# Moving a ScalarE weight split behind the next round's exponentials in a fused two-block transformer kernel

## The reference

```
h = rms_norm(x); z = h @ w_in                       # 1024 -> 5632
o_a = dilated_mixer(...)    # 6 heads, three dilations, softmax over a window
o_b = moba_attn(...)        # 6 heads, causal softmax
o_m = memory_attn(...)      # 4 heads on 256 memory tokens
gates = sigmoid(z[..., o3:])                        # 3 x 1024 columns of z
y = gates[0]*(o_a @ w_pa) + gates[1]*(o_b @ w_pb) + gates[2]*(o_m @ w_pm)
x = x + y @ w_o
x = x + square(relu(rms_norm(x) @ w_up)) @ w_down
```

## Time and profile before

| | |
|---|---|
| median of three runs | 1693.78 us |
| the profiled execution's own time | 1697.58 us |
| its span, first to last instruction | 1695.8 us |
| TensorE busy | 1516.9 us, 89% of the span |
| GpSimd busy | 601.3 us, 35% |
| ScalarE busy | 525.9 us, 31% |
| VectorE busy | 487.8 us, 29% |
| mean granted TensorE clock | 0.963 of full speed |
| attention rounds, first layer | from 97.99 to 195.65 us |
| attention rounds, second layer | from 520.67 to about 620 us |

### The profile page before, as it was taken

One profiled execution on the slowest core, in us unless ns is written; L12 is line 12 of the kernel. 1 busy time (PEld: TensorE's weight loads), 2 busy tenths in 40 slices (PEclk: granted clock), 3 DMA queues, 4 the chain that ended last, 5 costly groups with the idle time before them and its releaser, 6 DMA issues.

```text
span 1695.8 us, 17514 instructions
## 1 busy us (share of the span) xinstructions
PE 1516.9 (89%) x7436; PEld 1015.7 (60%) x7436; DVE 487.8 (29%) x803; ACT 525.9 (31%) x686; POOL 601.3 (35%) x167
## 2 busy tenths in 40 slices
PE   6999999999999999999999999989987676687666
PEld 4776678877777667887788887657742131131111
DVE  2222333331122233333243445577510000000001
ACT  5255353433425525344344333355210000000000
POOL 4655187734565518774346673010000000000000
PEclk9999999999999999999999999899999999898988
DMA  6534355598453335559825443000799999999996
GB/s 238 187 119 131 125 174 177 180 335 301 147 175 124 125 124 174 175 179 371 296 71 181 149 144 116 1 15 1 303 411 423 422 421 422 421 420 422 420 422 285
DMA packets 125497, 395.39 MB, mean 233 GB/s; under 512 B 6743, under 2 KB 10644, under 8 KB 101228
## 3 DMA queue, kind: packets, MB, share of 16 engines
q1 hardware_dynamic: 123536, 388.66, 62.0%
q0 software_dynamic: 1456, 4.52, 0.8%
q10 hardware_dynamic: 428, 1.10, 0.2%
HBM read 393.19 MB, written 1.05 MB: 232 GB/s over the span
## 4 chain that ended last, share of the span: by engine, by line
PE 70%; DMA 23%; DVE 2%; ACT 2%; issue 1%; SPq 1%; DVEq 0%; ACTq 0%
PE psum L1990 16%; PE psum L1992 16%; PE psum L1991 16%; DMA ring<-in_w_e_down 6%; PE psum L1982 4%; PE psum L1069 4%; DMA arena<-in_w_e_gate 3%; DMA ring<-in_w_e_gate 3%; DMA arena<-in_w_e_up 3%; DMA ring<-in_w_e_up 3%; DMA ring<-in_w_in 2%; DMA hT<-in_w_e_down 2%; DMA hT<-in_w_e_up 2%; PE psum L2221 1%; PE psum L983 1%
## 5 line engine op out<-in xcount | busy, mean ns | idle before, releaser
L593 POOL TENSOR_TENSOR ring_lo<-ring,ring_hi 128x2048 fp32r<-128x2048 f32 x101 | 467.8, 4636 | 367.0 <-ACT ring_hi L574 367.0
L1990 PE MATMUL psum<-ring_hi,hT_lo 128*128 128x512 f32 (+2 forms) x896 | 361.1, 403 | 13.2 <-DVE hT_lo L2239 10.5
L1992 PE MATMUL psum<-ring_hi,hT_hi 128*128 128x512 f32 (+2 forms) x912 | 357.4, 392 | 0.0
L1991 PE MATMUL psum<-ring_lo,hT_hi 128*128 128x512 f32 (+2 forms) x912 | 355.5, 390 | 0.0
L574 ACT ACTIVATE ring_hi<-ring 128x2048 fp32r<-128x2048 f32 x116 | 222.0, 1915 | 385.7 <-DMA ring<-in_w_in 123.2
L1069 PE MATMUL psum<-arena 128*32 128x512 f32 x740 | 166.1, 690 | 60.2 <-DMA arena<-in_w_e_gate 22.1
L1069 PE MATMUL psum<-ring,arena 128*32 128x512 f32 x708 | 159.6, 683 | 56.9 <-DMA ring<-in_w_e_gate 20.6
L1990 PEld LDWEIGHTS psum<-ring_hi,hT_lo 128*128 128x128 f32 x896 | 169.7, 189 | 55.1 <-DVE hT_lo L2239 11.9
L1992 PEld LDWEIGHTS psum<-ring_hi,hT_hi 128*128 128x128 f32 x912 | 172.9, 190 | 38.4
L1991 PEld LDWEIGHTS psum<-ring_lo,hT_hi 128*128 128x128 f32 x912 | 173.6, 190 | 34.1 <-issue 0.5
L1069 PEld LDWEIGHTS psum<-arena 128*32 128x32 f32 x740 | 35.9, 123 | 161.6 <-issue 50.9
(11 more groups left out here) (395 smaller groups left out, 1656.4 us busy)
## 6 DMA issues: line engine op xcount, KB each, us to landing
ring<-in_w_in SPq DMA_DIRECT2D x60, 1024.0 KB, 5.2
ring<-in_w_up SPq DMA_DIRECT2D x32, 1024.0 KB, 5.6
ring<-in_w_down SPq DMA_DIRECT2D x32, 1024.0 KB, 5.9
arena<-in_w_e_gate SPq DMA_DIRECT2D x31, 1024.0 KB, 26.8
arena<-in_w_e_up SPq DMA_DIRECT2D x31, 1024.0 KB, 27.0
ring<-in_w_e_gate SPq DMA_DIRECT2D x30, 1024.0 KB, 26.7
ring<-in_w_e_up SPq DMA_DIRECT2D x29, 1024.0 KB, 26.8
ring<-in_w_e_down SPq DMA_DIRECT2D x29, 1024.0 KB, 27.0
```

Source lines behind the costliest of these rows:

```text
L593: eng.tensor_tensor(slot_lo(u), slot(u), slot_hi(u).bitcast(F32), ALU.subtract).then_inc(done, 1)
L1990: pe.matmul(dst, lo(k0 + k), w_hi, start=start and k == 0, stop=False)
L1991: pe.matmul(dst, hi(k0 + k), w_lo, start=False, stop=False)
L1992: last = pe.matmul(dst, hi(k0 + k), w_hi, start=False, stop=stop and k == nk - 1)
```

## The change

In ScalarE's loop over the rounds the high part moves from the end of a round to a place inside the next round: behind the exponentials, the tanhs and the `PT` copy, and ahead of the `oT` copy. Unit 15 moves from round 0 to round 1, unit 16 from round 1 to round 2, and so on to unit 23 from round 8 to round 9. Nothing is added or removed: the same nine high parts per layer are made, in the same order. No other engine's program changes.

```
                     gates(gate_parts(j, 1))
                     if j >= 1:
+                        if 14 + j < 24:
+                            split_hi(act, l, 14 + j)
                         rows = slice(job["heads"][0][0], job["heads"][-1][0] + HD)
                         act.wait_ge(o_full, l * NJ + j)
                         act.activation(oT[rows, job["out"], job["t"] * P:(job["t"] + 1) * P], flat[2][rows, 768:768 + P],
                                        ACT.Copy).then_inc(o_sb, 1)
-                    if 15 + j < 24:
-                        split_hi(act, l, 15 + j)
```

## The result

| | before | changed |
|---|---|---|
| median of 14 runs each | 1695.19 us (1692.59 to 1698.05) | 1702.03 us (1698.34 to 1707.11) |
| ratio, 95% interval | | 1.0044 [1.0036, 1.0053] |
| the profiled execution's own time | 1697.58 us | 1702.03 us |
| its span | 1695.8 us | 1700.2 us |
| VectorE busy | 487.8 us | 520.4 us |

The account below looks back on a forecast made before the run. TensorE's program plus its pauses, where it waits for ScalarE, was taken to bound the attention stages. Pauses +5.9 and clock +1.6 (carried as +7.4) on the 1693.8 median gave about 1701 us; own range 1698 to 1706, whole range 1695.5 to 1708.

Parts of the forecast that it names:

- the pauses: Attention rounds: new TensorE pauses of 6.2 us per layer replace old ones of 3.2, +5.9 us for both layers.
- the clock: Attention stages: two falls of TensorE's clock in place of one, at 1.6 us a fall, +1.6 us.
- The hold of `nmx`: Rounds 3, 4, 6, 7, 8, 10: GpSimd's running low part holds VectorE's two-column `nmx`, 2.1 to 4.3 us, delaying exponentials.
- Rounds 3 to 5, 9 and 10: Round 3 held but hidden; 4 held, losing 1.31 us; 5 and 9 free; 10 held, losing 0.1 us.
- rival 2: Rounds 4, 7, 8: low parts lead too little; round 7 passes, others partly relieved; +2.2 us, 1696.0; 12%.
- The moved high parts and `oT` copies cost nothing: ScalarE: same high-part work; low parts stay far ahead of use; `oT` copies wait up to 1.9 us, transposes come 2.8 later.
- rival 1: ScalarE's order alone decides: `nmx` not held, old pauses and the clock fall go, -8.0 us, 1685.8; 8%.
- The sign: Attention rounds: slower by the two-port locking rule, though ScalarE's order alone would give a gain; slower 0.81, same 0.11, faster 0.08.

Follow-up runs that it names:

- second set: Follow-up timing of the unedited changed kernel beside the kernel before, in five rounds: ratio 1.0029, median 1701.3 us.
- one-column `nmx`: Changed kernel with `nmx` made by one 128x1 instruction per head instead of one for two columns: ratio 0.9949, 1687.2 us.
- low parts behind `nmx`: Changed kernel, two-column `nmx` kept, GpSimd's low parts of units 15 to 23 wait until the next job's `nmx` is through: 0.9949, 1686.5 us.
- high part at the end of the round: Kernel before with each high part one round later, at the round's end behind the `oT` copy, in both layers: 0.9947, 1687.0 us.
- four variants near 0.995: Changed with `nmx` per head (0.9949) or low parts held back (0.9949); high parts at round's end with two-column `nmx` (0.9947) or `nmx` per head (0.9952).
- the repeat: Changed kernel timed again without any edit, against the kernel before: ratio 1.0029, 1701.3 us.
- the last variant: The change made in the first of the two layers only, against the kernel before: ratio 1.0020, 1698.7 us.

## Why the prediction was right

The forecast was about 1701 us, +7.4 on 1693.8. The runs give +7.5 by the ratio (+6.8 by the medians), and in the second set +5 (+5.7). The mechanism was right; of the two terms of the sum, the pauses (+5.9) came out slightly larger, and the clock (+1.6) is not borne out. By its steps:

- **The hold of `nmx`.** Right, and shown: either the one-column `nmx` or the low parts behind `nmx` take the hold away, and the loss goes with it. The lengths came out within 0.1 us in the second layer. No exponential of the changed kernel's attention rounds stands behind a high part that waits for a transfer.
- **Rounds 3 to 5, 9 and 10.** As forecast: 3 held and hidden, 5 and 9 free, 10 held with no pause listed.
- **The pauses.** Forecast 1.31, 1.97, 1.47, 1.32 and 0.1 us, 6.2 us in all; listed in the second layer are 1.47, 1.81, 1.48, 1.25 and none, 6.0. The forecast counts late starts, and a listed pause is shorter than one: with the prediction's own allowances (0.17 us ahead of part 24, 0.06 ahead of products) the 6.0 are 6.4. Per layer the stage grew by 3.2 us, forecast 3.0.
- **The near misses** (rival 2) did not pass. Leads of 0.35, 0.43 and 0.32 us held, shorter than the 0.50 of the earlier trace rows; forecast were 0.31, 0.39 and 0.27.
- **The moved high parts and `oT` copies cost nothing.** Shown by the one-column `nmx` and by the low parts behind it (both 0.9949), which keep the changed order on ScalarE and have stages as short as the high part at the end of the round, in front of which the `oT` copy stays (94.25 to 94.30 us in all three).
- **The gain that the hold hides** (rival 1, -8.0 us). The one-column variant has it: -8.4 us in the medians. Its stages are 3.3 us shorter each than those of the kernel before with the same `nmx`, in which no clock fell (94.28 and 94.26 against 97.57 and 97.56); forecast were 3.2. None of the four variants near 0.995 has a fall in its attention stages, in one profile each.
- **The sign.** It can be read from the earlier trace rows alone. The Trainium skill (SBUF — State Buffer, Who interferes with whom) states that of GpSimd and a VectorE instruction in a two-port mode the first to issue has the shared ports for its whole instruction, and the other blocks fully. The traces agree: all 41 two-column `nmx` that were requested inside a low part, in the profiles of the two kernels, the repeat and the change in one layer, end 0.01 to 0.03 us behind it.
- **The clock: the term that was wrong.** I had two falls for one, +1.6 us at 1.6 us a fall. In these profiles the falls did become more frequent, but their price was taken as fixed, and it is not. The five falls in the profiled attention stages:

| stage | pause ahead of the fall, us | `nmx` of the next round | length, and without a fall, us |
|---|---|---|---|
| before, second layer | 1.77, round 8 | held 0.83 us | 99.34, 97.66 |
| changed again, first layer | 1.48, round 4 | free | 102.42, 100.85 |
| changed, first layer | 1.82, round 6 | held 3.16 us | 100.81, 100.85 |
| changed again, second layer | 1.82, round 6 | held 2.69 us | 100.85, 100.85 |
| changed in the first layer only, first layer | 1.81, round 6 | held 3.16 us | 100.84, 100.85 |

That is four falls in five profiled stages of the changed order, against one in five of the old order (two each of the kernel before and of the one with one-column `nmx`, and the second layer of the last variant), but three of the four cost nothing. The timeline of the changed kernel's first layer shows how this can be: matmuls listed with 0.63 us in place of 0.39, the `nmx` of round 7, and then the products of round 7, with no wait listed:

```profile
151.58 0.63 PE L1991 MATMUL psum<-ring_lo,hT_hi 128*128 128x512 f32 x1
152.01 0.63 PE L1992 MATMUL psum<-ring_hi,hT_hi 128*128 128x512 f32 x1
...
154.59 3.16 DVE L2388 TENSOR_SCALAR nmx<-mx 128x2 f32<-128x2 f32 x1
...
159.20 0.66 PE L2135 MATMUL psum<-arena 128*64 128x128 f32 x8
```

TensorE, slowed, came to round 7's scores late: `nmx` was requested 1.46 us into the low part (153.13 to 157.72) and not 0.4. But it ends with the low part all the same, 58.7 us into the stage, as it does in the second layer without a fall (58.8), and the exponentials with it. The lost time fills the pause of 1.48 us that this round has in the second layer. Behind round 4, and behind round 8 in the old order, the next round has no pause that could be filled, and those stages are 1.6 and 1.7 us longer. This is read from single profiles and was not put to a test.

In the profiles at hand the clock thus costs about as much in the old order (1.7 us in one stage of five) as in the changed one (1.6 in one of five), and what is left of the loss is the pauses: 3.2 to 3.3 us per layer, about 6.5 in all. This is an estimate from stages without a fall; it lies between the +5 and the +7.5 of the two sets. That the forecast of +7.4 came so near to the first of them is in part luck, as the term of 1.6 us in it is not seen. The profiles cannot settle the rest: outside the attention stages their spans vary from 1495.1 to 1500.5 us from one execution to the next, and no run was made to force or forbid a fall.

Two slips of the sum change nothing: 5.9 + 1.6 is 7.5 and was carried on as 7.4, and four falls give 1704.5 by the prediction's own prices, not the 1706 of its range.

## What to carry to other kernels

Before an instruction is moved on one engine, look at what its completion starts on another, and at whose instructions that one can hold: here a 0.17 us instruction on the critical path was stretched to 4.3 us by a 4.6 us one whose result was not needed until later. A duration that varies from round to round, and ends with another engine's instruction to within 0.03 us, is the sign to look for. The variants at 0.995 that keep the two-column `nmx` have both: the wait for the load out of the way (a unit is split a round later), and the long GpSimd instruction started behind the short VectorE one.

## What was not expected of the hardware

A lead of 0.32 us of the GpSimd instruction is enough to hold a two-column `nmx` for its whole length (585.37 against 585.69), while a one-column `nmx` was not held at any lead, down to 0.16 us. And a fall of the clock can cost nothing: where the slower matmuls fill a pause that was there anyway, the stage takes 100.81 us with a fall and 100.85 without; elsewhere one cost 1.6 us.
